# Expert loop of a PEER layer in groups of four chunks: four U groups, then output sums over four chunks in PSUM

## What is computed

```python
def chunk(args):
    xc, ec, gc = args
    act = jax.nn.gelu(jnp.einsum('cd,chkd->chk', xc, u_tab[ec]), approximate=False)
    return jnp.einsum('chk,chkd->cd', gc * act, v_tab[ec])
...
h = h + peer_ffn(rms_norm_2(h, norm_ffn[l]), peer_wq[l], peer_subkeys[l], peer_u[l], peer_v[l])
return rms_norm_2(h, norm_final)
```

## Time and profile before

| what | value |
|---|---|
| median of 3 runs | 3263.44 us (3259.84 to 3268.82) |
| profiled execution, its span | 3260.1 us |
| PE busy in the span | 2930.6 us (90%) |
| DVE, ACT, POOL busy | 1527.9, 1192.4, 1390.9 us |
| mean granted TensorE clock | 0.948 of full speed |
| expert loop, first U matmul to last output matmul | 1851.95 to 3239.00 us from the span's start |

### The profile page before, as it was taken

One profiled execution on the slowest core, in us unless ns is written; L12 is line 12 of the kernel. 1 busy time (PEld: TensorE's weight loads), 2 busy tenths in 40 slices (PEclk: granted clock), 3 DMA queues, 4 the chain that ended last, 5 costly groups with the idle time before them and its releaser, 6 DMA issues.

```text
span 3260.1 us, 37759 instructions
## 1 busy us (share of the span) xinstructions
PE 2930.6 (90%) x13578; PEld 2379.5 (73%) x13578; DVE 1527.9 (47%) x2861; ACT 1192.4 (37%) x1567; POOL 1390.9 (43%) x550
## 2 busy tenths in 40 slices
PE   7957899998989999789566799999999999999997
PEld 5723687876876678668455688888888888888885
DVE  2197521222155605469999643433443344334434
ACT  3244422222144522342377733333333333333331
POOL 5490354544310044423288744443444344434441
PEclk9978899998988999899788999999999999999998
DMA  3200122223210023211044743333333333333331
GB/s 131 78 0 1 52 90 90 103 77 143 91 40 1 1 90 114 86 59 65 13 117 141 213 154 127 111 116 129 128 110 116 129 123 115 116 129 125 113 103 45
DMA packets 185451, 308.51 MB, mean 95 GB/s; under 512 B 7072, under 2 KB 138528, under 8 KB 174368
## 3 DMA queue, kind: packets, MB, share of 16 engines
q1 hardware_dynamic: 185376, 307.56, 27.5%
HBM read 271.88 MB, written 35.65 MB: 94 GB/s over the span
## 4 chain that ended last, share of the span: by engine, by line
PE 80%; DVE 11%; issue 3%; ACT 2%; POOL 2%; DMA 1%; SPq 0%; DVEq 0%; POOLq 0%; ACTq 0%
PE bank L254 24%; PE bank L255 24%; PE bank L256 24%; DVE cacc L433 2%; DVE hits L1943 2%; PE bank L1163 2%; PE bank L1134 2%; PE bank L1800 1%; POOL ab L1610 1%; PE bank L1143 1%; DVE xl L397 0%; DVE one_hot L1914 0%; PE bank L1743 0%; DVE nrm L389 0%; DMA w_raw<-w_small 0%
## 5 line engine op out<-in xcount | busy, mean ns | idle before, releaser
L246 POOL TENSOR_TENSOR w_lo<-w_raw,w_hi 128x2048 fp32r<-128x2048 f32 (+2 forms) x96 | 418.5, 4361 | 805.5 <-ACT w_hi L241 805.3
L1994 DVE TENSOR_TENSOR resid<-bank,resid 128x512 f32<-128x512 f32 x512 | 354.2, 692 | 741.1 <-PE bank L256 741.1
L1590 POOL TENSOR_TENSOR u_lo<-u_raw,u_hi 128x1024 fp32r<-128x1024 f32 x124 | 296.0, 2410 | 747.7 <-ACT u_hi L1586 747.7
L254 PE MATMUL bank<-xh,w_lo 128*128 128x512 f32 x1056 | 422.0, 400 | 38.5 <-DVE xl L397 18.0
L255 PE MATMUL bank<-xl,w_hi 128*128 128x512 f32 x1056 | 417.9, 396 | 0.0
L256 PE MATMUL bank<-xh,w_hi 128*128 128x512 f32 x1056 | 417.3, 395 | 0.0
L254 PE MATMUL bank<-h_hi,v_lo 128*128 128x512 f32 x1024 | 400.7, 391 | 9.6 <-issue 9.6
L255 PE MATMUL bank<-h_lo,v_hi 128*128 128x512 f32 x1024 | 400.1, 391 | 0.0
L256 PE MATMUL bank<-h_hi,v_hi 128*128 128x512 f32 x1024 | 400.0, 391 | 0.0
L254 PE MATMUL bank<-xh,u_lo 128*128 128x512 f32 x992 | 386.7, 390 | 5.6 <-POOL u_lo L1590 5.6
L255 PE MATMUL bank<-xl,u_hi 128*128 128x512 f32 x992 | 386.4, 390 | 0.0
(11 more groups left out here) (346 smaller groups left out, 4813.1 us busy)
## 6 DMA issues: line engine op xcount, KB each, us to landing
w_raw<-w_small SPq DMA_DIRECT2D x80, 1024.0 KB, 4.8
u_raw<-expert_u SPq DMA_DIRECT2D x128, 512.0 KB, 5.2
v_raw<-expert_v SPq DMA_DIRECT2D x128, 512.0 KB, 4.6
g_in<-g_scratch SPq DMA_DIRECT2D x64, 512.0 KB, 4.2
g_scratch<-stage SPq DMA_DIRECT2D x7, 4096.0 KB, 15.9
w_raw<-w_small SPq DMA_DIRECT2D x8, 768.0 KB, 4.1
w_raw<-w_small SPq DMA_DIRECT2D x8, 640.0 KB, 3.7
cmp_w<-cmp_w SPq DMA_DIRECT2D x2, 2048.0 KB, 9.4
```

Source lines behind the costliest of these rows:

```text
L246: pool.tensor_tensor(wl[g % 2][:, :n], raw[g % 2][:, :n], wh[g % 2][:, :n].bitcast(F32), ALU.subtract).then_inc(sem("lo_done"), 1)
L254: pe.matmul(out, al, bh, start=(k == 0), stop=False)
L1590: pool.tensor_tensor(lo[:, :, :], u_raw[n % 4][:, :, :], hi[:, :, :].bitcast(F32), ALU.subtract)\
L1994: dve.tensor_tensor(resid[:, m, :], att_bank[m % 4][:, :], resid[:, m, :], ALU.add)\
```

## The change

The two halves of a quad become one. PE does four U groups (96 matmuls), then one `outputs` over four chunks: for each of 8 column blocks 12 matmuls into one bank. DVE adds 8 banks to the residual in a quad, not 16; the 256 additions fewer are the only instructions that the change removes, apart from bookkeeping. The number of matmuls is the same.

The other engines are put in an order that fits this. ACT waits once a quad for `out_done` of the quad before, then does `h_hi` and `v_hi` of the four chunks in turn, then gelu and the next `u_hi` in turn. POOL does four `v_lo`, then four `u_lo`. The splits of U run one quad further ahead: chunks 4 to 7 are split ahead of the loop, chunks 8 to 11 in its first pass. SP loads in a quad two gates, four V, four U. DVE does the 8 additions, then `weighted` of the next four chunks.

```diff
@@ peer_loads (SP)
             sp.wait_ge(sem("g_stored1"), 16 + 16 * QT)
+            for s in range(4):
+                load_u(sp, 0, s + 8)
 
             def quad(i, last):
+                for b in range(2):
+                    load_g(sp, i, b)
                 for s in range(4):
                     load_v(sp, i, s)
-                    if not last:
-                        load_u(sp, i, s + 4)
-                    if s % 2 == 0:
-                        load_g(sp, i, s // 2)
+                if not last:
+                    for s in range(4):
+                        load_u(sp, i, s + 8)
@@ block3_act
-            def quad(i, last):
-                for n in (0, 2):
-                    if n:
-
-                        act.wait_ge(sem("g_stored1"), 16 + 16 * QT)
-                    if not last:
-                        for c in (n + 4, n + 5):
-                            split_u_hi(act, i, c, u_hi[c % 4])
...
+            def quad(i, more_gelu, more_u):
+
+                act.wait_ge(sem("out_done"), i * 8 + 8)
+                for s in range(4):
+
+                    act.wait_ge(sem("h_f"), i * 4 + (s + 5))
+                    act.activation(h_hi[s][:, :], h_raw[s][:, :], ACT.Copy).then_inc(sem("h_hi"), 1)
+                    act.wait_ge(sem(f"v_loaded{s}"), i * 16 + 16)
+                    act.activation(v_hi[s][:, :], v_raw[s][:, :], ACT.Copy).then_inc(sem("v_hi"), 1)
+                if more_gelu:
+                    for c in range(4):
+                        gelu(i, c + 4)
+                        if more_u:
+                            split_u_hi(act, i, c + 8, u_hi[c])
+
+            for c in range(4):
+                if c == 2:
+
+                    act.wait_ge(sem("g_stored1"), 16 + 16 * QT)
+                split_u_hi(act, 0, c + 4, u_hi[c])
@@ block3_pe
-            def outputs(i, b):
-
-                pe.wait_ge(sem("v_lo"), i * 4 + (2 * b + 6))
-                pe.wait_ge(sem("h_lo"), i * 4 + (2 * b + 6))
+            def outputs(i):
+
+                pe.wait_ge(sem("v_lo"), i * 4 + 8)
+                pe.wait_ge(sem("h_lo"), i * 4 + 8)
...
             def quad(i, last):
-                for b in range(2):
-                    if not last:
-                        for n in (2 * b + 4, 2 * b + 5):
-                            activations(i, n, u_hi[n % 4], u_lo[n % 4])
-                    outputs(i, b)
+                if not last:
+                    for n in range(4, 8):
+                        activations(i, n, u_hi[n % 4], u_lo[n % 4])
+                outputs(i)
@@ block3_dve
             def quad(i, last):
-                for b in range(2):
-                    add_outputs(i, b)
-                    if b == 0 or not last:
-                        weighted(i, 2 * b + 2)
-                        weighted(i, 2 * b + 3)
+                add_outputs(i)
+                if not last:
+                    for n in range(4, 8):
+                        weighted(i, n)
```

More of the change, by code:

```diff
@@ L1508, in peer_credits @@
             for name, n in (("pk_s", 4), ("pk_sc", 4), ("g_done", 4), ("g_free", 4), ("pk_t", 1), ("pk_idx", 1), ("g_stored0", 16), ("g_stored1", 16), ("a_rows", 4), ("b_rows", 4),
-                            ("u_lo", 4), ("v_lo", 4), ("ge", 4), ("out_done", 16), ("out_free", 4), ("h_f", 4), ("h_lo", 4)):
+                            ("u_lo", 4), ("v_lo", 4), ("ge", 4), ("out_done", 8), ("out_free", 4), ("h_f", 4), ("h_lo", 4)):
                 pool.nop().then_inc(sem(name), n)
@@ L1612, in quad @@
             def quad(i, last):
-                for n in (0, 2):
-                    if not last:
-                        for c in (n + 4, n + 5):
[L1616 to L1622, removed]
+                for s in range(4):
+                    pool.wait_ge(sem("v_hi"), i * 4 + (s + 1))
+                    pool.tensor_tensor(v_lo[s][:, :], v_raw[s][:, :], v_hi[s][:, :].bitcast(F32), ALU.subtract)\
+                        .then_inc(sem("v_lo"), 1)
+                if not last:
+                    for c in range(8, 12):
+                        split_u_lo(pool, i, c, u_hi[c % 4], u_lo[c % 4])
+            for c in range(4, 8):
+                split_u_lo(pool, 0, c, u_hi[c % 4], u_lo[c % 4])
+            with pool.Fori(0, QUADS - 2) as i:
                 quad(i, False)
+            quad(QUADS - 2, True)
             quad(QUADS - 1, True)
@@ L1696, in block3_act @@
             store_rows(QT - 1, True)
-            def quad(i, last):
-                for n in (0, 2):
-                    if n:
-                        act.wait_ge(sem("g_stored1"), 16 + 16 * QT)
-                    if not last:
-                        for c in (n + 4, n + 5):
-                            split_u_hi(act, i, c, u_hi[c % 4])
[L1706 to L1723, removed]
+            def quad(i, more_gelu, more_u):
+                act.wait_ge(sem("out_done"), i * 8 + 8)
+                for s in range(4):
+                    act.wait_ge(sem("h_f"), i * 4 + (s + 5))
[11 more added lines that the diff above has]
+                split_u_hi(act, 0, c + 4, u_hi[c])
+            with act.Fori(0, QUADS - 2) as i:
+                quad(i, True, True)
+            quad(QUADS - 2, True, False)
+            quad(QUADS - 1, False, False)
+            act.wait_ge(sem("out_free"), 4 + 8 * QUADS)
             for k in range(KD):
@@ L1808, in block3_pe @@
             pe.wait_ge(sem("g_free"), 4 + QT * BG)
-            def outputs(i, b):
-                pe.wait_ge(sem("v_lo"), i * 4 + (2 * b + 6))
-                pe.wait_ge(sem("h_lo"), i * 4 + (2 * b + 6))
+            def outputs(i):
+                pe.wait_ge(sem("v_lo"), i * 4 + 8)
+                pe.wait_ge(sem("h_lo"), i * 4 + 8)
                 for m in range(KD):
-                    pe.wait_ge(sem("out_free"), i * 16 + (8 * b + m + 1))
+                    pe.wait_ge(sem("out_free"), i * 8 + (m + 1))
                     cols = slice(m * P, (m + 1) * P)
-                    pairs = [(v_hi[s][:, cols], v_lo[s][:, cols], h_hi[s][:, :], h_lo[s][:, :]) for s in (2 * b, 2 * b + 1)]
+                    pairs = [(v_hi[s][:, cols], v_lo[s][:, cols], h_hi[s][:, :], h_lo[s][:, :]) for s in range(4)]
                     products(pe, att_bank[m % 4][:, :], pairs).then_inc(sem("out_done"), 1)
             def quad(i, last):
-                for b in range(2):
-                    if not last:
-                        for n in (2 * b + 4, 2 * b + 5):
-                            activations(i, n, u_hi[n % 4], u_lo[n % 4])
-                    outputs(i, b)
+                if not last:
+                    for n in range(4, 8):
+                        activations(i, n, u_hi[n % 4], u_lo[n % 4])
+                outputs(i)
             with pe.Fori(0, QUADS - 1) as i:
@@ L1988, in weighted, with add_outputs @@
                    .then_inc(sem("h_lo"), 1)
[L1990 removed]
+            def add_outputs(i):
                 for m in range(KD):
[L1993 removed]
+                    dve.wait_ge(sem("out_done"), i * 8 + (8 + m + 1))
                     dve.tensor_tensor(resid[:, m, :], att_bank[m % 4][:, :], resid[:, m, :], ALU.add)\
@@ L1997, in quad @@
             def quad(i, last):
-                for b in range(2):
-                    add_outputs(i, b)
-                    if b == 0 or not last:
-                        weighted(i, 2 * b + 2)
-                        weighted(i, 2 * b + 3)
-            weighted(0, 0)
-            weighted(0, 1)
+                add_outputs(i)
+                if not last:
+                    for n in range(4, 8):
+                        weighted(i, n)
+            for n in range(4):
+                weighted(0, n)
             with dve.Fori(0, QUADS - 1) as i:
```

3 lines of the change are left out of this document (2 added, 1 removed).

## The result

The changed kernel takes 3283.99 us (median, 3282.27 to 3293.22), the kernel before 3263.12 us (3259.84 to 3268.82, with one run more of it than stood above): ratio of the runs 1.0073, 95% interval 1.0055 to 1.0091 (the two medians divided give 1.0064, which lies in it). The forecast was 3285 us, range 3272 to 3296. The profiled execution has a span of 3282.2 us, 22.1 more than before.

What follows compares the result with a forecast made beforehand. PE, busy without a gap in the loop, was taken as the bound, so only the ends count: head 17.8 plus tail 3.8, 21.6 us on a 3260.1 us span, gives 3281.7, a median of 3285 us; range 3272 to 3296.

Steps and rivals of the forecast that it cites:

- The middle, worth 0: Middle of the loop: the operand chain stays covered by PE's U groups, worth 0, with 5 us to spare.
- The cover of 21.8 us: Each quad in the middle: PE's four U groups, 96 matmuls, last 21.8 us while the next outputs' operands are made.
- The blocking of DVE and POOL: Operand chain: DVE and POOL instructions wait for whole ones of each other, POOL 2.4 us, DVE some 0.5.
- B at 3221.97: Operand chain: the start of DVE's first product, from which the steps were counted; forecast 1.04 us behind the last output matmul's start.
- The head, +17.8: First quad: PE waits for chunk 6 behind G's store, then 4.4 us before outputs; +17.8 us, from +12.4 to +22.8.
- the restart behind the shorter wait: Head: slow clock after PE's 4.4 us wait ahead of the first outputs, put at 1.0 us.
- The tail, +3.8: Last quad: one wait of 16.7 us and one restart of 2.2 replace two waits and two restarts; +3.8 us.
- A: Rival at head and tail: both lose, but DVE and POOL hardly meet; about 3276 us, chance 0.13.
- B: Rival in the middle: the chain is not covered and PE waits every quad; 3325 us, chance 0.07.
- C: Rival for PE's pace: not slower, longer matmul runs and fewer DVE PSUM reads speed it; 3260 us, chance 0.03.
- D: Rival: change not as described, or ends overlap otherwise; within 10 us, 3268 us, chance 0.05.
- the three waits: PE gaps: 10 to 12 us ahead of U near 1874.5, 3 to 5 before first outputs, 16 to 17 in the tail.

Runs made afterwards that it cites:

- v_lo_small: The changed kernel with POOL computing `v_lo` for only 64 of 1024 columns from the second quad on; 3275.17 us, one run.
- tail_v_early: The changed kernel with the last quad's `v_hi` and `v_lo` made during the outputs of the quad before; 3277.14 us, ratio 1.0053 to the kernel before.
- v_lo_plus2: The changed kernel with two more POOL subtractions of 2048 columns ahead of the fourth `v_lo` in every quad; 3480.27 us, one run.
- v_lo_plus1: The changed kernel with one more POOL subtraction of 2048 columns ahead of the fourth `v_lo` in every quad; 3296.42 us, one run.
- adds_twice: The changed kernel with each residual addition preceded by one into a spare tile, so DVE does 512 again; 3284.21 us, ratio 1.0066 to the kernel before.
- tail_halves: The changed kernel with the outputs of its last quad alone in two halves on PE and DVE; 3281.33 us, ratio 1.0064 to the kernel before.
- ends_mended: The changed kernel with its first quad in two halves and the last quad's operands made a quad early; 3247.89 us, ratio 0.9958 to the kernel before.
- before_tail: The kernel before with only its tail mended, the last quad's operands made ahead into free buffers; 3247.95 us, ratio 0.9959 to the kernel before.

## Why the prediction was right

**The middle, worth 0.** 43.52 us a quad in both kernels, to the hundredth over 29 quads. The cover of 21.8 us is shown by the two kernels with more POOL work, not only by the absence of a wait.

**The blocking of DVE and POOL.** The chain was stepped as one instruction waiting for a whole one of the other engine. In the tail, counted from B at 3221.97, the four `v_lo` ended at 4.93, 7.67, 12.42 and 15.17 us; stepped were 5.0, 7.9, 12.7 and 15.6. That POOL is the cause is shown by v_lo_small and tail_v_early. The first blocked `h_lo` of the tail ended at 5.48, 0.55 us behind the end of the first `v_lo`. The additions, with one SBUF input, took 0.69 us beside POOL's `u_lo` (1892.44 to 1901.87) as without it (at 1896.70 and 1910.32). So the Trainium skill's rule ("SBUF — State Buffer", section "Who interferes with whom") is borne out for two SBUF inputs and for one.

**The head, +17.8.** Measured 18.13. The store released ACT at 1871.15 (1870.93 taken), PE restarted at 1874.76 (1874.55), the outputs at 1892.07 (1892.05). Counted from the last matmul of G, which came 0.46 us later than before, the outputs began 0.44 us earlier than forecast. The term mis-sized the other way is the restart behind the shorter wait: set at 1.0 us, between none and a full one, it was full, 1.73 us (23.49 us from 1892.07 to 1915.56 for 96 matmuls that need 21.76). Together they make the +0.3. v_lo_plus2 shows a restart behind a wait of 3.87 us from start to start in all of 30 quads.

**The tail, +3.8.** Measured 2.92: the wait was 16.26 and not 16.7 us, and the restart cost 1.78 and not 2.2. The stepping took a `v_lo` blocked by DVE at 2.9 us from the end of the one before it, and 2.75 was measured, twice (4.93 to 7.67, 12.42 to 15.17).

**The rivals.** A (no blocking) would have been 3276 us and fell: the profile shows the blocked instructions, and the two kernels without them have the 9.2 to 9.8 us wait. B fell with the profile after, where PE has no wait in the middle; v_lo_plus1 shows that this was no near thing. C fell with adds_twice and with the pace: 0.2266 us with groups of 12 as with groups of 6. D (within 10 us) fell with the time, 20.9 us between the medians, and with the three waits, which stand where they were forecast.

That the total came within 1 us is in part luck: head and tail were off by +0.3 and -0.9 us, 1.0 us of the profile's difference lies outside both, and the forecast put 3.3 us between span and median, where the result has 1.8 (3282.2 to 3283.99). The mechanism doesn't rest on that luck.

## What to carry to other kernels

Where one engine is busy without a gap, read a change of order at the two ends of the loop first: there the work that covered a wait is missing, and a coarser group makes the uncovered chain longer. Ask for each member of the group whether it needs something that lands late; one late member holds the whole group (chunk 6 here, 11 us). A tail without cover was mended here by making the last group's operands a step early in buffers whose last use is over: 14.9 us of the tail. Nothing that was tried inside the loop made the kernel faster.

## What the runs showed of the hardware beyond what was expected

Each of the 30 waits of 3.87 us in v_lo_plus2 was followed by 7 to 14 steps from matmul to matmul of over 0.35 us, most of them 0.427, where 0.2267 is usual. The shortest wait in an expert loop with such steps behind it is one of 3.84 us in the head of tail_halves (1885.99 to 1889.83), which cost 2.7 us. In the kernel before the shortest was 5.2 us. The waits of 0.81 us in ends_mended and 1.73 us in before_tail had none, and no expert loop of these kernels has a wait in between. The granted clock was still 1.00 in v_lo_plus2 during the wait itself (2044.5 to 2047.9 us) and 0.53, close to its lower level of 1.2 GHz, in the 3.6 us behind it. So a repeated wait of 3.65 us cost 5.9 us in the mean.

The price of such a restart isn't one number. In v_lo_plus2 it goes up and down from quad to quad, some 1.7 us and then some 2.9, so that quads of some 48.9 and some 50.1 us alternate through the whole loop though the wait is the same to 0.01 us. Over all twelve profiles a restart behind a wait costs 1.5 to 2.9 us, with no relation to the length of the wait (1.5 us behind 9.06 us, 2.7 behind 3.84). What sets it was not looked into.
